# One recurrent layer's output product: who scales its weights, and in which order they are used

## What is computed

```python
r = jax.nn.sigmoid(ga)
i = jax.nn.sigmoid(gi)
log_a = -LRU_C * r * jax.nn.softplus(-lam)
a = jnp.exp(log_a)
u = jnp.sqrt(-jnp.expm1(2.0 * log_a)) * (i * x)      # then a scan: h[t] = a[t] h[t-1] + u[t], both directions
y = (forward + backward) * jax.nn.gelu(gate, approximate=True)
return y @ w_out                                     # 1024 x 1024; then RMSNorm, residual, the second feed-forward block
```

## Time and profile before

| | us |
|---|---|
| median of 3 runs | 718.25 (717.76 to 718.87) |
| profiled execution, whole | 717.85 |
| its span | 716.0 |
| PE busy in the span | 704.6 |
| DVE busy | 607.3 |
| ACT busy | 520.2 |
| POOL busy | 25.0 |

### The profile page before, as it was taken

How to read it: one execution, slowest core, us unless ns; L and a number is a source line. 1 busy time by engine, 2 the same in 40 slices (tenths; PEclk the granted TensorE clock), 3 DMA queues, 4 the chain that set the end, 5 groups by cost and what they waited for, 6 DMA issues and landing times.

```text
span 716.0 us, 16121 instructions
## 1 busy us (share of the span) xinstructions
PE 704.6 (98%) x6542; PEld 589.9 (82%) x6542; DVE 607.3 (85%) x820; ACT 520.2 (73%) x848; POOL 25.0 (3%) x28
## 2 busy tenths in 40 slices
PE   9999999999999999999999999999899999999996
PEld 6788787878899888888889998888788888885464
DVE  6969877777889799989898889898999999999643
ACT  7566675857576789778777677899668888988431
POOL 0010010101010000000002300000000000000000
PEclk9999999999999999999999999999999999999999
DMA  9873363452683356555589963100525666766821
GB/s 309 318 234 120 119 235 119 166 188 104 211 274 121 111 192 225 192 195 200 176 264 388 370 216 117 62 1 1 196 98 190 224 206 207 233 211 207 275 43 59
DMA packets 106396, 132.08 MB, mean 184 GB/s; under 512 B 12385, under 2 KB 74337, under 8 KB 106209
## 3 DMA queue, kind: packets, MB, share of 16 engines
q1 hardware_dynamic: 105904, 130.97, 54.4%
q10 hardware_dynamic: 432, 0.31, 0.2%
HBM read 129.17 MB, written 1.05 MB: 182 GB/s over the span
## 4 chain that ended last, share of the span: by engine, by line
PE 82%; DVE 8%; ACT 6%; DMA 2%; issue 1%; SPq 1%; DVEq 0%
PE ps L1653 22%; PE ps L1655 22%; PE ps L1654 22%; PE ps L2036 3%; PE ps L2037 3%; PE ps L2035 3%; DMA stage<-in_ret_w_in 2%; PE ps L1696 1%; PE ps L1700 1%; PE ps L1695 1%; DVE a_lo L1082 1%; SPq L495 1%; PE ps L1901 1%; DVE hT L1098 1%; DVE w_lo L1036 1%
## 5 line engine op out<-in xcount | busy, mean ns | idle before, releaser
L1653 PE MATMUL ps<-a_hi,w_hi 128*128 128x272 f16 (+1 forms) x1000 | 276.9, 277 | 0.1
L1654 PE MATMUL ps<-a_lo,w_hi 128*128 128x272 f16 (+1 forms) x1000 | 276.9, 277 | 0.0
L1655 PE MATMUL ps<-a_hi,w_lo 128*128 128x272 f16 (+1 forms) x1000 | 276.9, 277 | 0.0
L1036 DVE SCALAR_TENSOR_TENSOR w_lo<-stage,w_hi 128x1024 f16<-128x1024 f32 x207 | 246.5, 1221 | 34.3 <-ACT w_hi L579 34.0
L579 ACT ACTIVATE w_hi<-stage 128x1024 f16<-128x1024 f32 x207 | 208.5, 1044 | 30.6 <-PE ps L2037 18.3
L1653 PEld LDWEIGHTS ps<-a_hi,w_hi 128*128 128x128 f16 x1000 | 97.8, 98 | 17.3 <-DVE rs L1045 0.9
L1655 PEld LDWEIGHTS ps<-a_hi,w_lo 128*128 128x128 f16 x1000 | 97.8, 98 | 16.0
L1654 PEld LDWEIGHTS ps<-a_lo,w_hi 128*128 128x128 f16 x1000 | 97.8, 98 | 15.7
L1653 PE MATMUL ps<-y_hi,w_hi 128*128 128x272 f16 (+3 forms) x496 | 106.1, 242 | 0.0
L1654 PE MATMUL ps<-y_lo,w_hi 128*128 128x272 f16 (+3 forms) x496 | 106.1, 242 | 0.0
L1655 PE MATMUL ps<-y_hi,w_lo 128*128 128x272 f16 (+3 forms) x496 | 106.0, 242 | 0.0
(11 more groups left out here) (278 smaller groups left out, 1104.2 us busy)
## 6 DMA issues: line engine op xcount, KB each, us to landing
stage<-in_ffn_w_in SPq DMA_DIRECT2D x96, 512.0 KB
stage<-in_ffn_w_out SPq DMA_DIRECT2D x24, 1024.0 KB
stage<-in_ret_w_in SPq DMA_DIRECT2D x16, 1024.0 KB
stage<-in_ret_w_out SPq DMA_DIRECT2D x8, 1024.0 KB
...
```

Source lines behind the costliest of these rows:

```text
L1036: dve.scalar_tensor_tensor(out=part(1, c, q), in0=flat(stage, c, q), scalar=W_SCALE, in1=part(0, c, q), op0=ALU.mult, op1=ALU.subtract).th ...
L1653: pe.matmul(o, w_h, x_h, start=start, stop=False)
L1654: pe.matmul(o, w_h, x_l, start=False, stop=False)
L1655: return pe.matmul(o, w_l, x_h, start=False, stop=stop)
```

## The change

Four things are done together.

- POOL makes the high halves of the two output chunks (eight tensor_scalar of 128 x 1024, `pool_high`), which ACT made before. They stand behind `sum_parts(1)` in POOL's list and wait for the landed weights and for the place they write. The wait counts of later chunks are kept by one larger increment (`counted`).
- POOL makes 1 - p for all four blocks (`a_made`), in place of DVE (blocks 0, 1) and ACT (blocks 2, 3). The arrays of block 0 move to mT, those of blocks 2 and 3 to the place of the second gate chunk, so that `block_exps(2)` waits for the last gate product.
- The second output chunk lies in the third weight buffer (`w_hi_third`, with `decay_all` for its low half), which XR1 used before it. Its quarters are loaded in another order, and PE uses them in another: high halves first, low halves of the weights last. DVE makes the low halves of LRU_OUT later than before and three of the second chunk's after the last block's `lru_y`.
- ACT loads the Gelu table earlier, scales the two tiles of the output (`out_scaled`) in place of DVE, and converts FFN1_IN's quarters from an earlier place in its list.

```diff
@@ -241,15 +241,16 @@
-        lr = [quad(decay_all, 0), quad(y_lo_f32, 2), quad(y_lo_f32, 1), quad(g0_place, 2)]
-
-        li = [quad(decay_all, 1), quad(y_hi_f32, 2), quad(y_hi_f32, 1), quad(l_place, 0)]
-
-        la = [quad(g0_place, 0), quad(g0_place, 1), quad(decay_all, 0), quad(decay_all, 1)]
+        lr = [quad(mT_flat, 0), quad(y_lo_f32, 2), quad(y_lo_f32, 1), quad(g0_place, 2)]
+
+        li = [quad(mT_flat, 1), quad(y_hi_f32, 2), quad(y_hi_f32, 1), quad(l_place, 0)]
+
+        la = [quad(g0_place, 0), quad(g0_place, 1), quad(g1_place, 0), quad(g1_place, 1)]
...
@@ -264,7 +265,7 @@
+                     GT0: (y_hi_flat[:, 0:KC * CW], y_lo_flat[:, 0:KC * CW]), LRU_OUT + 1: third}
 
...
@@ -528,10 +539,11 @@
-                    rows_k = lru_w_out[0].rearrange("(k p) n -> p k n", p=P)[:, k:k + 2, :]
+                    quarters = [(2 * half, 0), (2 * half, 1)] if n == 0 else [(0, half), (2, half)]
                     to = half_slot(LRU_OUT + n, half)
-                    return [(to[:, 2 * m:2 * m + 2, :], rows_k[:, :, m * CW:(m + 1) * CW]) for m in range(2)]
+                    return [(to[:, 2 * at:2 * at + 2, :],
+                             lru_w_out[0].rearrange("(k p) n -> p k n", p=P)[:, 4 * n + k:4 * n + k + 2, m * CW:(m + 1) * CW])
...
@@ -570,13 +582,12 @@
                 elif c == FFN1_IN + 1:
-                    act.wait_ge(w_used, used(XR1))
-                elif c == LRU_OUT + 1:
-                    act.wait_ge(gates_up, 8)
+                    act.wait_ge(w_used, used(LRU_OUT + 1))
...
@@ -879,8 +888,8 @@
-                if blk >= 2:
-                    act.wait_ge(scanned, 1)
+                if blk == 2:
+                    act.wait_ge(gates_up, 8)
...
@@ -897,11 +906,6 @@
-            def block_decay(blk):
-                act.wait_ge(q_made, blk + 1)
-                act.wait_ge(scanned, 2)
-                act.activation(a_late[blk], la[blk], ACTF.Copy, scale=-1.0, bias=1.0).then_inc(a_made, 1)
-
...
@@ -932,6 +934,7 @@
             block_root(1)
+            act.activation(est_warm[:], eps_sb[:], ACTF.Gelu_apprx_tanh)
             gates(4)
             gates(5)
...
             block_root(2)
-            block_decay(2)
             block_root(3)
-            prep(LRU_OUT + 1, 0)
             gate_gelu(1)
-            prep(LRU_OUT + 1, 1)
+            prep(LRU_OUT + 2, 0)
             lru_y(2)
-            block_decay(3)
-            prep(LRU_OUT + 1, 2)
-            prep(LRU_OUT + 1, 3)
-            for q in range(SUB - 1):
+            for q in range(1, SUB - 1):
                 prep(LRU_OUT + 2, q)
             lru_y(3)
             load_estimate_table()
             prep(LRU_OUT + 2, 3)
-            out_squares(LRU_OUT + 1, 2, 0, T0_LRU_OUT, 2)
...
+            def out_scaled(n):
+
+                act.activation(mT[:, n, T0_LRU_OUT:T], ps[:, X + n, T0_LRU_OUT:T], ACTF.Copy,
+                               scale=gain(5, n)).then_inc(m_scaled, 1)
+
+            out_squares(LRU_OUT + 1, 2, 0, T0_LRU_OUT, 1)
+            out_scaled(0)
+            out_square(LRU_OUT + 1, 2, 1, 0, T0_LRU_OUT)
+            out_scaled(1)
+            for n in range(1, 4):
+                out_square(LRU_OUT + 1, 2, 1, n, T0_LRU_OUT)
             estimate(STAT, T0_LRU_OUT, ms_up, MEAN[("post", 2)], ESTIMATE[("post", 2)])
             norm_input(3, T0_LRU_OUT, (4, 6))
...
@@ -1026,7 +1034,10 @@
 
-                dve.wait_ge(whi_made, SUB * c + q + 1 + 2 * SUB * i)
+                if c in (LRU_OUT, LRU_OUT + 1):
+                    dve.wait_ge(pool_high, highs(c, q))
+                else:
+                    dve.wait_ge(whi_made, SUB * c + q + 1 + 2 * SUB * i)
...
@@ -1489,59 +1493,57 @@
             x_evict(0)
-            prep(LRU_OUT, 1)
...
             x_low(0, 1)
-            prep(LRU_OUT, 2)
...
-            v, a, both = {}, {}, {}
+            both = {}
             gated = {0: gated_x(0)}
-            prep(LRU_OUT, 3)
+            prep(LRU_OUT, 0)
             x_low(1, 0)
             x_low(1, 1)
+            prep(LRU_OUT, 1)
             lru_q(0)
-            v[0] = lru_v(0, gated[0])
-            a[0] = lru_a(0)
+            lru_v(0, gated[0])
             gated[1] = gated_x(1)
...
             lru_y(0, both[0])
             lru_y(1, both[1])
             gated[2] = gated_x(2)
+            prep(LRU_OUT, 3)
             gated[3] = gated_x(3)
+            prep(LRU_OUT + 1, 0)
             lru_q(2)
-            v[2] = lru_v(2, gated[2])
+            lru_v(2, gated[2])
             lru_y_low(0)
             lru_y_low(1)
             gate_evict(1)
             lru_q(3)
-            v[3] = lru_v(3, gated[3])
-            both[2] = lru_scan(2, lru_drive(2, v[2]))
-            prep(LRU_OUT + 1, 0)
+            lru_v(3, gated[3])
+            both[2] = lru_scan(2, lru_drive(2))
             lru_y(2, both[2])
-            driven = lru_drive(3, v[3])
+            driven = lru_drive(3)
             lru_y_low(2)
-            prep(LRU_OUT + 1, 1)
             both[3] = lru_scan(3, driven)
             lru_y(3, both[3])
+            prep(LRU_OUT + 1, 1)
+            lru_y_low(3)
             prep(LRU_OUT + 1, 2)
-            lru_y_low(3)
             prep(LRU_OUT + 1, 3)
             prep(LRU_OUT + 2, 0)
             prep(LRU_OUT + 2, 1)
             dve.wait_ge(m_sq, 2 * DT + 4)
             dve.tensor_tensor(sq[:, 0:2, T0_LRU_OUT:T], sq[:, 0:2, T0_LRU_OUT:T], sq[:, 2:4, T0_LRU_OUT:T],
                               ALU.add).then_inc(sum_m, 1)
-            out_scale(2, T0_LRU_OUT)
             prep(LRU_OUT + 2, 2)
             prep(LRU_OUT + 2, 3)
...
@@ -1645,6 +1647,20 @@
+
+            for c in (LRU_OUT, LRU_OUT + 1):
+                for q in range(SUB):
+                    pool.wait_ge(w_landed[c % 2][q // 2], landed(c))
+                    pool.wait_ge(w_used, freed(c, q) if c == LRU_OUT else used(XR1))
+                    pool.tensor_scalar(part(0, c, q), flat(stage, c, q), W_SCALE, None, ALU.mult).then_inc(pool_high, 1)
+
+            for blk in range(LRU_BLOCKS):
+                if blk < 2:
+                    pool.wait_ge(v_made, blk + 1)
+                else:
+                    pool.wait_ge(q_made, blk + 1)
+                    pool.wait_ge(scanned, 2)
+                pool.tensor_scalar(a_late.get(blk, la[blk]), la[blk], -1.0, 1.0, ALU.mult, ALU.add).then_inc(a_made, 1)
...
@@ -2007,13 +2023,59 @@
+            def late_product(w, y, blk, half, m, stop=False):
+
+                for kk in range(2):
+                    k, at = 2 * blk + kk, 4 * half + 2 * (blk - 2) + kk
+                    mm = pe.matmul(ps[:, (X, Y)[half] + m, T0_LRU_OUT:T], w[:, at, m * P:(m + 1) * P],
+                                   y[:, k, T0_LRU_OUT:T], start=False, stop=stop and kk == 1)
+                return mm
+
+            def late_products(w, y, blk, half):
+
+                for m in range(4):
+                    late_product(w, y, blk, half, m)
+
+            pe.wait_ge(yhi_made, Y_LRU + 3)
+            pe.wait_ge(wlo_made, SUB * (LRU_OUT + 1) + 1)
+            late_products(wh, y_hi, 2, 0)
+            late_products(wl, y_hi, 2, 0)
+            pe.wait_ge(pool_high, highs(LRU_OUT + 1, 2))
+            late_products(wh, y_hi, 2, 1)
+            pe.wait_ge(ylo_made, HEADS + 3)
+            late_products(wh, y_lo, 2, 0)
+            late_products(wh, y_lo, 2, 1)
+            pe.wait_ge(yhi_made, Y_LRU + 4)
+            late_products(wh, y_hi, 3, 0)
+            pe.wait_ge(pool_high, highs(LRU_OUT + 1, 3))
+            late_products(wh, y_hi, 3, 1)
+            pe.wait_ge(wlo_made, SUB * (LRU_OUT + 1) + 2)
+            late_products(wl, y_hi, 3, 0)
+            pe.wait_ge(ylo_made, HEADS + 4)
+            for m in range(4):
+                mm = late_product(wh, y_lo, 3, 0, m, True)
+                if m < 3:
+                    mm.then_inc(bank_up, 1)
+            mm.then_inc(w_used, 2)
+            for m in range(4):
+                late_product(wh, y_lo, 3, 1, m)
+                if m == 0:
+                    pe.wait_ge(wlo_made, SUB * (LRU_OUT + 1) + 3)
+                late_product(wl, y_hi, 2, 1, m)
+                if m == 0:
+                    pe.wait_ge(wlo_made, SUB * (LRU_OUT + 1) + 4)
+                mm = late_product(wl, y_hi, 3, 1, m, True)
+                if m < 3:
+                    mm.then_inc(bank_up, 1)
+            mm.then_inc(w_used, 2)
             pe.wait_ge(sum_m, 5)
             for dt in (0, 1, 4, 5, 6, 7):
                 mean_part(2, T0_LRU_OUT, dt, start=dt == 0)
```

More of the change, by code:

```diff
@@ L430, in weights, with counted, highs @@
             return w_hi[RING_RANK[c] % 2], w_lo[RING_RANK[c] % 2]
+        def counted(c, q):
+            return 2 * SUB + 1 if (c, q) == (FFN1_IN, 0) else 1
+        def highs(c, q):
+            return SUB * (c - LRU_OUT) + q + 1
         block = ctx.enter_context(nc.Block())
@@ L1059, in out_scale @@
             def out_scale(i, t0):
-                for dt in range(4 if i < 2 else 2):
+                for dt in range(4):
```

(2 more changed lines are left out.)

60 lines of the change are left out of this document (25 added, 35 removed).

## The result

The changed kernel takes 720.53 us in the median of nine runs (720.01 to 721.15); the kernel before 717.77 us, also of nine. The ratio is 1.0036, with a 95% interval of 1.0026 to 1.0046: 1.9 to 3.3 us slower. The forecast was 721.0 us.

A forecast was written before the change was run, and what follows sets the result against it. PE, busy 704.6 of 716.0 us, was taken as the bound. 717.85 + 2.4 (norm chain) + 0.4 (recurrence) = 720.65 us, plus 0.4 to the median: forecast 721.0 us, range 715.4 to 727.0.

The forecast's parts named there:

- First place: Norm chain, 423 to 434 us: POOL's first four scalings cost DVE 3.0 us and make PE 2.4 us late.
- the sign was 2 to 3: Between 423 and 437 us: PE would wait 2 to 3 us in all for `a_lo`, and none before.
- Second place: Recurrence: four scalings and four 1 - p cost DVE 7.0 us, mostly hidden; PE's products end 0.4 us later.
- DVE's idle time of 5.6 us: Recurrence, 448.3 to 507.7 us: DVE's idle time in the kernel before, counted as room for the second place's cost.
- The new order pays only if y comes earlier: Output product: 56 products behind the last y, not 48; gain 2.2 us with y at 505.8, loss 0.4 at 508.4.
- The length of a scaling: POOL's 1024-column scaling: taken as 0.87 us from a memset's slope, range to 2.15, and charged to DVE in full.
- the sign that I had set for it: POOL's scalings in the changed profile: 1.4 us or more in a calm stretch would mean the dearer scaling.
- the rival of the dearer scaling: Norm chain and recurrence: a scaling takes 1.4 us, 727.4 us, chance 0.13; or 2.15 us, 736.4 us, chance 0.05.
- its second half: In that rival: DVE loses a scaling's whole length, so the longer scaling raises the cost at both places.
- the row in which DVE had lost 0.57 us: Kernel before, from 391.52 us: four DVE low halves took 5.19 us instead of 4.62 beside POOL's sums.

The follow-up runs named there:

- run 2: Changed kernel with POOL's first four scalings replaced by memsets of the same place, which read nothing: 718.35 us, 1.0008 of the kernel before.
- run 6: Changed kernel with ScalarE again making the first output chunk's four high halves, at its old places: 718.15 us, 1.0002 of the kernel before.
- runs 1 and 4: Changed kernel, first four scalings held until the norm chain ends: 720.34 us; then also the second four until the convolution's second input is out: 720.4 us.
- run 9: run 6 with the 1 - p of blocks 2 and 3 moved from GpSimd to ScalarE: 716.99 us, 0.9986 of the kernel before.
- run 10: run 9 with the 1 - p of block 0 on VectorE and of block 1 on ScalarE: 716.57 us, 0.9981 of the kernel before.
- run 11: run 10 with VectorE's low half of the second chunk's first quarter ahead of its wait for the last gates: 716.51 us, 0.9980.
- run 12: run 11 with the second chunk block by block, its second low half earlier, 48 products behind the last y instead of 56: 715.6 us, 0.9963.
- run 5: Changed kernel with all eight high-half scalings on GpSimd replaced by memsets: 717.77 us, 0.9995 of the kernel before.
- run 8: Changed kernel with all eight high halves on ScalarE, two 1 - p each on VectorE and ScalarE, none on GpSimd: 719.28 us, 1.0018.

## Why the prediction was right

The forecast was 0.5 us from the result, and both its terms can be read in the trace. Yet one of its inputs was far off, and the time came out in spite of it.

*First place, +2.4 us: right.* DVE lost 2.94 us in the norm chain (3.0 forecast), PE's end of XR1 came 2.33 us late (2.4), the scalings began at 423.0, and PE waits for `a_lo` where it had not (1.31 us as the profile counts them, where the sign was 2 to 3; the delay of 2.33 lies in that range). That 3.0 came out is partly luck: I had charged 0.87 us four times less 0.52 for idle time and one-input instructions, and the trace has 0.74 four times and takes only 0.07 back (the last `a_lo` is 2.87 us late). Two errors of about 0.5 us cancel. Runs 2 and 6, which take the reading or the instructions away, give back 2.0 and 2.4 us. What I had not seen is that the place hardly matters: by runs 1 and 4 PE follows DVE as closely up to the gates, and moving the four instructions by 12 us changed nothing.

*Second place, +0.4 us: made up as I said, and smaller.* The last y came with the same distance to XR1 (0.09 us less, 0.2 more forecast), 0.85 us went into eight products more, and 0.55 came back from the wait for a low half: 0.21 us. DVE's idle time of 5.6 us was what hid POOL's instructions, and it is down to 0.6. "The new order pays only if y comes earlier" fits runs 9 to 12, though none of them has the old order: with the 1 - p off GpSimd the last y comes earlier (506.64 in run 11 against 508.67 in run 6, 1.8 us when the 0.3 us of run 6 are taken off), and with the eight products ahead of it again run 12 is 0.39% or 2.8 us faster than run 6.

*The length of a scaling: wrong.* I took 0.87 us for the whole instruction from the fill's slope. It is 2.8 us, outside my own bounds of 0.87 to 2.15, since none of the rows I had wrote float16 from float32 with a reading. By the sign that I had set for it (1.4 us or more in a calm stretch), the rival of the dearer scaling would hold, with 727 or 736 us. It didn't, because its second half is wrong: I had made the length of POOL's instruction and the loss of DVE one number. DVE lost 0.65 to 0.84 us to each scaling of 2.8 us and 0.77 to 0.90 to each 1 - p of 1.1 us. Both are 0.6 to 0.8 ns a column, whatever the rest of the instruction does. The time was right because what I charged DVE was nearly right. That the two engines hold each other up at all rested on the row in which DVE had lost 0.57 us, and this held. The amount of 0.87 us did not come from there but from the slope of a fill, an instruction that by run 2 costs DVE nothing: that 0.85 ns a column lies near the 0.6 to 0.8 that DVE lost is luck. The Trainium skill, "SBUF — State Buffer", sections "SBUF: two separate sides" and "Who interferes with whom", has the two engines exclude each other for the whole instruction; this trace agrees that they do, and that a fill doesn't take part, but not on the length: 0.7 of 2.8 us.

*Smaller points.* I charged the second place eight instructions at 0.87, 7.0 us. The four scalings cost 0.69 + 0.76 + 1.33 = 2.8 us (the rows at 448.03, 451.70 and 453.10, the last against its 5.62 us in run 5) and the four 1 - p 0.89 + 0.77 + 0.90 + 0.90 = 3.5 us, together 6.2 us. Of the scalings' part 1.56 us only filled a wait for ACT (run 5); the last two 1 - p stood on the path, with 1.1 us by run 9. PE has no wait for a low half of the weights in the changed kernel, as forecast. ACT, which I had counted as no longer setting the pace, is what DVE waits for as soon as POOL takes less from it: 1.56 us in run 5, 0.98 in run 10, 0.65 in run 11.

What stays open is the new order by itself: run 8 mixed it with ScalarE's late high halves, and the 0.85 - 0.55 us are read from traces, not from a kernel with that edit alone.
